# SSM taps and SSM output with even and odd channel groups alternating in the two row halves of TensorE, one core

## The reference

```python
ug = u.astype(jnp.float32).reshape(b, L, SSM_GROUPS, SSM_GROUP)      # 32 groups of 16 channels
bu_re = jnp.einsum('blgc,gpc->blgp', ug, bbar_re)                    # 64 complex states per group
...
_, _, h_re, h_im = lax.associative_scan(_cplx_combine, (a_r, a_i, bu_re, bu_im), axis=1)
y = (jnp.einsum('blgp,gcp->blgc', h_re, c_re.astype(jnp.float32))
     - jnp.einsum('blgp,gcp->blgc', h_im, c_im.astype(jnp.float32))
     + d_skip.astype(jnp.float32).reshape(SSM_GROUPS, SSM_GROUP) * ug)
```

## Time and profile before

| | |
|---|---|
| time, median of 3 runs | 946.68 us (944.63 to 947.23) |
| the profiled execution | 947.71 us, its span 946.0 us |
| mean granted TensorE clock | 0.887 |
| TensorE matmul busy | 816.3 us (86%) |
| VectorE, ScalarE, GpSimd busy | 301.0, 189.4, 166.6 us |
| moved by DMA | 272.69 MB, 288 GB/s over the span |

### The profile page before, as it was taken

The page is one execution under the profiler, slowest core; times in us unless marked ns, Lnnn a source line. Parts: engine busy times, 40 slices in busy tenths (PEclk is TensorE's granted clock), DMA queues, the critical chain, the costliest instruction groups (busy, mean ns, idle before and its releaser), DMA issues.

```text
span 946.0 us, 14967 instructions
## 1 busy us (share of the span) xinstructions
PE 816.3 (86%) x5066; PEld 528.8 (56%) x5067; DVE 301.0 (32%) x660; ACT 189.4 (20%) x419; POOL 166.6 (18%) x303
## 2 busy tenths in 40 slices
PE   5999896999999999389997897797999999999740
PEld 3555483877655456256655454455666666666430
DVE  2589468421224323432221111121222222122117
ACT  3000033222233012102221111111122221222103
POOL 3029985000001000021110101010111111110021
PEclk9999995565579999589999989899999999999975
DMA  9974003520375043949999999999999987999976
GB/s 362 398 298 40 1 2 37 188 101 0 75 310 196 11 178 118 391 159 420 418 420 419 420 418 422 419 421 417 421 417 422 406 332 285 419 421 417 419 255 259
DMA packets 66218, 272.69 MB, mean 288 GB/s; under 512 B 19384, under 2 KB 22328, under 8 KB 43760
## 3 DMA queue, kind: packets, MB, share of 16 engines
q1 hardware_dynamic: 55024, 251.25, 67.3%
q0 software_dynamic: 4480, 10.67, 3.1%
q10 hardware_dynamic: 6688, 10.42, 3.0%
HBM read 241.38 MB, written 35.14 MB: 292 GB/s over the span
## 4 chain that ended last, share of the span: by engine, by line
PE 57%; DMA 14%; SPq 8%; DVE 8%; POOL 6%; issue 4%; ACT 2%; POOLq 0%; DVEq 0%
PE pair L913 15%; PE pair L935 8%; PE pair L761 8%; DMA reg_f<-in_w_exp_up 7%; DMA slot<-in_w_exp_up 7%; PE pair L663 3%; PE pair L604 3%; PE pair L914 3%; SPq L327 3%; SPq L330 2%; PE pair L695 2%; PE pair L661 2%; PE pair L817 2%; SPq L320 1%; PE pair L718 1%
## 5 line engine op out<-in xcount | busy, mean ns | idle before, releaser
L913 PE MATMUL pair<-slot,probs 128*64 128x256 f32 x800 | 185.8, 393 | 26.6 <-DMA slot<-in_w_exp_up 24.9
L914 PE MATMUL pair<-slot,probs 128*64 128x256 f32 x800 | 186.1, 393 | 0.0
L913 PEld LDWEIGHTS pair<-slot,probs 128*64 128x64 f32 x800 | 112.9, 142 | 79.8 <-issue 46.3
L1555 DVE TENSOR_TENSOR probs<-pair,probs 64x256 f32<-64x256 f32 x74 | 31.5, 426 | 314.8 <-ACT probs L1116 218.7
L914 PEld LDWEIGHTS pair<-slot,probs 128*64 128x64 f32 x800 | 113.0, 142 | 0.0
L541 POOL DMA_INDIRECT probs<-hf_scr,row_u x38 | 40.6, 1067 | 406.3 <-DVE row_u L1503 405.6
L913 PE MATMUL pair<-reg_h,probs 128*64 128x256 f32 x384 | 89.5, 394 | 10.5 <-DMA reg_f<-in_w_exp_up 10.5
L935 PE MATMUL pair<-slot,sums 128*64 128x512 f32 x400 | 91.4, 597 | 4.6 <-ACT sums L1120 4.6
L914 PE MATMUL pair<-reg_f,probs 128*64 128x256 f32 x384 | 89.6, 394 | 0.0
L604 PE MATMUL pair<-reg_h,slot 128*128 128x512 f32 x160 | 83.7, 606 | 2.4 <-DVEq L1217 2.4
L913 PEld LDWEIGHTS pair<-reg_h,probs 128*64 128x64 f32 x384 | 54.3, 143 | 36.8 <-issue 21.6
(11 more groups left out here) (356 smaller groups left out, 1096.4 us busy)
## 6 DMA issues: line engine op xcount, KB each, us to landing
slot<-in_w_exp_gate SPq DMA_DIRECT2D x22, 2048.0 KB, 23.5
slot<-in_w_exp_up SPq DMA_DIRECT2D x22, 2048.0 KB, 27.5
slot<-in_w_exp_down SPq DMA_DIRECT2D x44, 1024.0 KB, 24.2
reg_h<-in_w_exp_gate SPq DMA_DIRECT2D x10, 2048.0 KB, 24.5
reg_f<-in_w_exp_up SPq DMA_DIRECT2D x10, 2048.0 KB, 29.2
y_slots<-probs_t SPq DMA_DIRECT2D x1, 13312.0 KB, 45.0
y_slots<-sums ACTq DMA_DIRECT2D x74, 128.0 KB, 6.5
reg_h<-in_w_exp_down SPq DMA_DIRECT2D x10, 512.0 KB, 23.8
```

The source lines that it names most:

```text
L913: pe.matmul(gu[j][0:TT], lhs, gate_w[q][:, h, c, out], start=n == 0, stop=n == KD - 1)
L914: ins = pe.matmul(gu[j][TT:P], lhs, up_w[q][:, h, c, out], start=n == 0, stop=n == KD - 1)
L1555: tt(hid[:, part], gu[j], act_g[:, part], ALU.mult)\
```

## The change

`kernels` and `ssm_out` take the pair number q (0 to 3) in place of h, and write both parities in one call. Within a pair of groups the two convolution matmuls come first, then the 64-row matmuls with even and odd group in turn. A call waits for both banks of the call before it (`2 * q`), and counts both up at its end. `BESIDE` now puts one call of eight groups into each of the units 3, 4, 5 and 6; before it was 12, 8, 8 and 4 groups. ScalarE copies the two banks one after the other.

```diff
-BESIDE = ((), (), (), (0, 1, 2), (3, 4), (5, 6), (7,), ())
+BESIDE = ((), (), (), (0,), (1,), (2,), (3,), ())
...
-            def kernels(h):
-
-                q, m = h // 2, h % 2
-                if h >= 2:
-                    pe.wait_ge(s["kern_out"], h - 1)
-                rows = slice(HD * m, HD * m + HD)
+            def kernels(q):
+
+                if q >= 1:
+                    pe.wait_ge(s["kern_out"], 2 * q)
                 for j in range(4):
                     r = 4 * q + j
-                    for i in range(2):
-                        pe.matmul(pp[2][0:GC, m, P * j:P * j + GC], bbar[rows, i, r, :], ssm_c[rows, i, r, :],
-                                  start=i == 0, stop=i == 1)
-                    for i in range(2):
-                        ins = pe.matmul(pp[2][0:GC, m, P * j + GC:P * j + P], bbar[rows, i, r, :],
-                                        out_tab[rows, r, i, 0:T - 1, :], start=i == 0, stop=i == 1)
-                ins.then_inc(s["kern_ps"], 1)
+                    for table, out in ((ssm_c, slice(P * j, P * j + GC)), (None, slice(P * j + GC, P * j + P))):
+                        for i in range(2):
+                            for m in range(2):
+                                rows = slice(HD * m, HD * m + HD)
+                                right = out_tab[rows, r, i, 0:T - 1, :] if table is None else table[rows, i, r, :]
+                                ins = pe.matmul(pp[2][0:GC, m, out], bbar[rows, i, r, :], right,
+                                                start=i == 0, stop=i == 1)
+                                if j == 3 and table is None and i == 1:
+                                    ins.then_inc(s["kern_ps"], 1)
...
-            def ssm_out(h):
-
-                q, m = h // 2, h % 2
-                if h >= 2:
-                    pe.wait_ge(s["y_out_done"], h - 1)
-                rows = slice(HD * m, HD * m + HD)
+            def ssm_out(q):
+
+                if q >= 1:
+                    pe.wait_ge(s["y_out_done"], 2 * q)
                 for j in range(4):
                     r = 4 * q + j
-                    t = pp[2][:, m, NC * j:NC * j + NC]
-                    pe.matmul(t, conv_w[:, 2 * r + m, :], u_c[:, 2 * r + m, :], start=True, stop=False)
+                    out = [pp[2][:, m, NC * j:NC * j + NC] for m in range(2)]
+                    for m in range(2):
+                        pe.matmul(out[m], conv_w[:, 2 * r + m, :], u_c[:, 2 * r + m, :], start=True, stop=False)
                     for i in range(2):
-                        ins = pe.matmul(t, out_tab[rows, r, i].rearrange("p t c -> p (t c)"), states[rows, r, i, :],
-                                        start=False, stop=i == 1)
-                ins.then_inc(s["y_ps"], 1)
+                        for m in range(2):
+                            rows = slice(HD * m, HD * m + HD)
+                            ins = pe.matmul(out[m], out_tab[rows, r, i].rearrange("p t c -> p (t c)"),
+                                            states[rows, r, i, :], start=False, stop=i == 1)
+                            if j == 3 and i == 1:
+                                ins.then_inc(s["y_ps"], 1)
```

More of the change, by code:

```diff
@@ L729, in squares @@
                 ins.then_inc(s["ssq_ps"], 1)
-            for h in range(8):
-                kernels(h)
+            for q in range(4):
+                kernels(q)
             scores(0)
@@ L741, in _ @@
                     squares(n // 2 - 1)
-                for h in BESIDE[n]:
-                    if h == 0:
+                for q in BESIDE[n]:
+                    if q == 0:
                         pe.wait_ge(s["conv_in"], 16 * T)
@@ L746, in _ @@
                         pe.wait_ge(s["states_done"], 3)
-                    ssm_out(h)
+                    ssm_out(q)
                 if n % 2:
@@ L1041, in _ @@
                 pt_copy(n)
-                for h in BESIDE[n]:
-                    ssm_copy(h)
+                for q in BESIDE[n]:
+                    ssm_copy(2 * q)
+                    ssm_copy(2 * q + 1)
                 if n + 2 < 8:
```

## The result

The change is faster: 923.43 us, median of 4 runs (917.78 to 924.88), against 946.17 us for four runs of the kernel before (944.63 to 947.23). The ratio is 0.9746, with a 95% interval of 0.9708 to 0.9784. Six more runs, made later beside an experiment (last of the experiments), gave a median of 918.81 us (912.02 to 925.82).

A forecast was written before the change was run, and what follows sets the result against it. TensorE was taken to bound the kernel in the SSM output, mostly at half clock. Shorter pairs, with the clock holding through units 4 and 5, save 27.9 us: 947.71 - 27.9 = 919.8, forecast 920 us, range 915 to 938.

The forecast's parts named there:

- The taps at nothing: Taps before the SSM output: three added waits of about 1.25 us stay under VectorE's 6.7 us cover, gain 0.
- The pair of groups: SSM output: a pair falls from 3.44 to 2.14 us at half clock, from 1.96 to 1.20 at full.
- The other bound: SSM output pair with no overlap of the halves at all: 2.98 us at half clock, 1.64 at full.
- The rival of program order: SSM pairs: matmuls start strictly in order, so the odd half starts one record late; 2.4 us less saved, 922.2; chance 0.10.
- The rival of no overlap: SSM output: halves run one after the other, only row-mode changes are saved, 6.9 us, 940.8; chance 0.05.
- The slower rival: SSM output and taps: a change of half costs like a change of row mode, nothing overlaps; 969 us; chance 0.04.
- The rival of no effect: Expert weight transfers set the end, so an earlier start only lengthens a wait; 947.7 us; chance 0.03.
- The walk: TensorE through units 3 to 6, summed stretch by stretch: end at 218.3 in place of 246.2, 27.9 us saved.
- Passed on whole: Behind the last SSM block, through GLU and experts: the whole 27.9 us saving reaches the kernel's end.
- I take the clock to hold through units 4 and 5: Granted clock rises to 1.00 near 190 us and stays, so SSM blocks there take 4.8 us each.
- clock as before: Rival: clock rises and falls where it did before, SSM blocks total 30.0 us, 19.1 saved, 928.6; chance 0.20.

The follow-up runs named there:

- e2: The taps of the change alone, with SSM output and table of the kernel before: 947.39 us, ratio 1.0011.
- e3: The changed kernel with each pair made of two groups of the same parity, so all eight 64-row records use one half: 941.92 us, ratio 0.9954.
- e4: The changed kernel with all four records of a pair's even group before the four of the odd one: 915.58 us, ratio 0.9665.
- e12: The changed kernel itself, unedited, run and profiled once more: 918.81 us over 6 runs, ratio 0.9697.
- e1: SSM output and table of the change, with the taps of the kernel before: 919.22 us, ratio 0.9735.
- e6: The changed kernel with its second call moved from unit 4 to unit 3, none in unit 4: 923.07 us, ratio 0.9753.
- e7: The changed kernel with the squares of unit 6 moved behind the last SSM block: 915.31 us, ratio 0.9648.
- e11: The changed kernel with half-by-half order in each pair and the squares of unit 6 behind the last SSM block: 914.87 us over 6 runs, ratio 0.9658.
- e8: The changed kernel with the weighted sum of unit 3 moved ahead of its SSM block: 926.12 us, ratio 0.971.

## Why the prediction was right

- **Forecast and range.** 920 us, 915 to 938, faster. The median is 923.43, that of the second set 918.81.
- **The taps at nothing: right.** The scores moved from 141.53 to 139.27 and VectorE's start behind the first tap not at all; e2 gives 1.0011. The three waits are 1.12 to 1.14 us, for a forecast of 1.25, and the overlapped block of 16 records takes 0.48 us.
- **The pair of groups: right to the hundredth.** 1.07 and 0.60 us were forecast for eight records in two halves, and measured. The other bound, 2.98 us for a pair without overlap, is what e3 measures (2.99). The price of a change of row mode, 0.23, is confirmed by the same run: 0.45 for two.
- **The rival of program order: refuted.** The Trainium skill's "TensorE: Matmul & The Clock Gate", Part 3, Packing small matmuls, has matmuls start and end in program order. For these 64-row matmuls the trace does not agree on the start: e4, which should suffer most from that order, kept 1.08 us per block, and its halves start together.
- **The rival of no overlap: refuted** by the change's own blocks of 1.07 us. What it would have cost is shown by e3, which is that case: 941.92 us, for the rival's 940.8, and 18.5 above the change's median of the first set. The slower rival fell with it. The rival of no effect fell too: the first expert matmul starts 29.7 us earlier, 1.0 of them from the earlier start.
- **The walk.** Unit 3 took 8.4 us for 8.6, units 4 and 5 4.7 each for 4.8, and the last block ended at 218.0; with the 1.0 us of earlier start taken out that is 219, for 218.3. Two terms were mis-sized. Unit 6's block took 8.0 us and not 6.7, since the clock fell in its first pair and not half way. The squares waited 0.49 us and not 0.9.
- **Passed on whole: right to the experts.** 27.3 us were won in the SSM stretch, 28.6 up to the GLU and up to the experts. The 3.2 us lost behind them need no cause in the edit: e2, with the old SSM output, shows 541.2 us there against the 538.2 of before.
- **The step that was right in the profile and wrong as a reason** is "I take the clock to hold through units 4 and 5". It did in the profiled run, and in e12, the same program, it did not: there it fell at 195.6. What the rival "clock as before" asked, I treated as a question that the order of the program decides. For this program it differs from run to run: e1, with the same SSM output, had it at 1.00 from 190.6 to 211.1, as the first profile had, and e12 did not. In e6 and e12 the total stayed near the forecast because time at half clock that is added in one stretch is partly missing in the next; e7 and e11 show no such exchange. From the first SSM matmul to the GLU they took 71.2 and 65.7 us, where the change took 76.0 and 75.6. That the median came within 3.4 us of the forecast is therefore in part luck: the change's ten runs spread over 13.8 us.

What stays open: what decides where the clock rises. e7 and e11, with the squares behind the last block, had it at full clock in unit 6; so had e12, without that edit. One profile each does not settle whether the late squares help. e8's clock that stayed low may be its early wait or its run.

## What to carry to other kernels

Where two sorts of matmul use half the rows each, put work for both halves into one block between two changes of row mode: here, with 64-row float32 matmuls of 80 columns, eight records in two halves cost what four in one cost, and neither of two orders inside the block was better. Price such a gain first with the clock where it was, stretch by stretch, check it in full-clock work (length times granted clock), and treat the clock's share as a spread, not as a term: here the work was 8.9 us less and the time 27.3, of which some 8 hang on where the clock rose and fell. Before reading a few us into an edit, look whether the unchanged program shows them from one profile to the next.

## What was not expected of the hardware

- The granted clock of one and the same program changes at different places in different runs (the change: 1.00 from 190.3 to 210.8 in one profile, from 188.8 to 195.6 and again from 216.1 in the other), and its ten runs reach from 912 to 926 us; before the change the mean clock kept to 0.884 to 0.892 over 43 runs.
- Four records queued for one half do not hold back the four behind them that go to the other half (e4: 1.08 us a block, with two records in its first 0.02 us).
- A stretch that ends late at half clock can be followed by one at a higher clock: 45.1 us at 0.65 and 30.5 at 0.89 (e12), against 40.8 at 0.75 and 35.2 at 0.74, come to the same sum within 0.4 us. It need not be so: 30.6 us at 0.99 were followed by 35.1 at 0.76 (e11).
